# Differential attention's queries and keys turned by VectorE and DMA through DRAM, scores in rounded halves

## The chip, the cores and the metric

The kernel runs on one core of a Trainium2 chip. The metric is the device time of one execution in microseconds; smaller is better. Shown is the median of three executions.

## The reference

Two layers over 512 positions of width 1024, batch 1, all in float32. The second one (dilated windows and latent attention) isn't touched. The first is a retention branch and a differential attention branch behind one projection `w_in` of 1024 x 9216:

```python
h = rms_norm(x, norm_g);  z = h @ w_in            # q_d, k_d: 1024 columns each
qd = rms_norm(q_d.reshape(B, S, 8, 2, 64), diff_q_norm_g)   # 8 heads, two maps of 64
kd = rms_norm(k_d.reshape(B, S, 8, 2, 64), diff_k_norm_g)
# for each head, each block i of 128 queries, keys up to the block's end:
s = (qd * 64**-0.5) . kd - slope_h * dist;  s = -inf where key > query
p = softmax(s);  a = p[map 0] - lam * p[map 1];  o = a @ v_d
```

Then each head's output is normalised, gated, multiplied by `diff_w_o` and mixed with the retention branch.

## The kernel before

Positions are split in four tiles of 128 (`TT`). All projections are one stream on TensorE: 35 groups of up to eight slabs, a slab being 128 rows of a weight by 512 columns. A weight comes by DMA in chunks of two slabs (`chunk`, SyncE's queue, two buffers `raw`), ScalarE rounds it (`hi`, line 574, `w_hi`, float32r) and GpSimd takes the rest (`lo`, line 943, `w_lo`), each three slabs ahead, with four split slots. A product is then three rounded matmuls (`mm3`, lines 1708 to 1710): high by high, high by low, low by high. One slab is four of them, one for each tile: four slots. Every engine has a program of its own, written out in order, and they meet at semaphores.

The attention stage is the seven groups 13 to 19 (`in_diff`), 56 slabs or 224 slots v. Groups 10 and 11 before it project queries and keys of heads 0 to 3, groups 14 and 15 those of heads 4 to 7. Normalising: GpSimd squares, VectorE sums, takes the root and scales (`head_scale`, line 1239). Attention is written as generators, one per engine, over blocks n = 4h + i (head h, query block i). `diff_due(v)` says how many steps have been taken by slot v, and each slot calls `next` as often as that grows. A block's chain: TensorE's scores (`scores`, line 1808; per map j an fp32 matmul of 64 rows, 128(i+1) wide), VectorE adds bias and takes the maximum (line 1415, `s_max`), ScalarE takes exponentials (line 736, `s_exp`), VectorE the reciprocal (line 1406, `s_inv`), GpSimd scales map 1 (line 1030, `s_scaled`), VectorE combines (line 1438, `s_comb`), TensorE turns the probabilities (`turn_probs`, line 1833), VectorE copies them out (line 1424), TensorE makes the outputs (`outputs`, line 1820). `scores(n + 1)` are issued in iteration n, the turn of n in iteration n + 2. Both maps have one PSUM bank each.

Queries and keys come to their turned form on TensorE: `diff_turn` transposes four 128x128 tiles of `z_sb` into bank `A[2]` (line 1793), once for a head's queries and once for its keys, and ScalarE evicts them with gain and scale (`diff_queries`, `diff_keys`, lines 719 and 724). Each has a step of its own in iterations i = 1 and 2 of the head before:

```python
DIFF_FIRST, DIFF_SECOND, DIFF_THIRD, DIFF_LAST = 10, 116, 160, 208
```

so 86 steps, 36 of them up to slot 115, 22 in the next 44 slots and 28 in the last 48.

## Time and profile before

| | us |
|---|---|
| median of 3 executions (lowest, highest) | 908.52 (908.18, 908.61) |
| the profiled execution | 908.68 |
| its span, first to last instruction | 906.9 |
| TensorE busy in it | 896.1 |
| VectorE, ScalarE, GpSimd busy | 423.1, 397.3, 439.2 |
| DMA | 81.29 MB, 43564 packets |

What lies between the profiled execution's time and its span (1.8 us) is start and end around the program. Busy time of TensorE includes pipelining: a matmul's end is modelled, and starts are closer together than durations, so costs on TensorE are read from start to start. Engines other than TensorE may overlap it entirely. The granted clock is 1.00 throughout (2.4 GHz).

### The profile page before, as it was taken

Reading aid. Unit: us, or ns where it says so; the run is one execution under the profiler, and the core shown is the slowest. Engines: PE = TensorE matmul, PEld = TensorE weight load, DVE = VectorE, ACT = ScalarE, POOL = GpSimd, SP = SyncE. Lnnn points to the kernel's source line nnn. Section 1 sums busy time; section 2 is a strip of 40 time slices with the busy share of each in tenths; the row PEclk is TensorE's granted clock in tenths of the full one; section 3 lists DMA queues with packets and bytes.
Section 4 is the critical chain, followed back from the end, with each engine's and each line's share of the span. In section 5 each row is a group of like instructions: output and inputs, shape, how many; then the busy total and the mean of one; then the engine's idle time right before and its main releaser. Section 6 shows DMA issues by size and latency. Waiting matters only on the chain.

```text
span 906.9 us, 12615 instructions
## 1 busy us (share of the span) xinstructions
PE 896.1 (99%) x4648; PEld 712.7 (79%) x4648; DVE 423.1 (47%) x957; ACT 397.3 (44%) x872; POOL 439.2 (48%) x376
## 2 busy tenths in 40 slices
PE   9999999999999999999999999999999998999998
PEld 7878888888888877777777788889888765777776
DVE  3221251545114413467474455646648866543631
ACT  5533323333223344454554444244435774655531
POOL 4544436445446654646444444545458382234362
PEclk9999999999999999999999999999999999999999
DMA  8442222313333332122222233233433321011113
GB/s 317 152 104 77 65 70 79 108 59 105 96 104 100 97 90 73 48 72 70 69 55 63 70 116 139 93 108 96 120 101 105 94 87 53 25 47 47 47 47 116
DMA packets 43564, 81.29 MB, mean 90 GB/s; under 512 B 4416, under 2 KB 6208, under 8 KB 43504
## 3 DMA queue, kind: packets, MB, share of 16 engines
q1 hardware_dynamic: 42016, 79.95, 29.3%
q8 instruction: 37, 0.61, 0.3%
q10 hardware_dynamic: 1488, 0.55, 0.3%
q14 instruction: 23, 0.19, 0.1%
HBM read 78.36 MB, written 2.12 MB: 89 GB/s over the span
## 4 chain that ended last, share of the span: by engine, by line
PE 84%; DVE 8%; issue 3%; POOL 2%; DMA 2%; ACT 1%; SPq 0%; ACTq 0%; DVEq 0%; POOLq 0%
PE Z L1708 23%; PE Z L1710 22%; PE Z L1709 22%; PE A L1885 3%; PE A L1808 2%; PE A L1923 2%; PE A L1894 2%; PE A L1820 2%; DMA raw<-in_w_in 2%; DVE z_sb L1239 1%; PE A L1868 1%; POOL w_lo L943 1%; DVE rstd L1142 1%; PE A L1833 1%; PE A L1718 1%
## 5 line engine op out<-in xcount | busy, mean ns | idle before, releaser
L943 POOL TENSOR_TENSOR w_lo<-raw,w_hi 128x512 fp32r<-128x512 f32 (+1 forms) x262 | 345.3, 1325 | 443.9 <-ACT w_hi L574 442.6
L574 ACT CAST w_hi<-raw 128x512 fp32r<-128x512 f32 (+1 forms) x262 | 157.9, 614 | 293.7 <-PE Z L1710 259.7
L1708 PE MATMUL Z<-w_hi,hT_hi 128*128 128x512 f32 (+1 forms) x544 | 217.8, 400 | 0.1
L1710 PE MATMUL Z<-w_hi,hT_lo 128*128 128x512 f32 (+1 forms) x544 | 211.3, 388 | 0.0
L1709 PE MATMUL Z<-w_lo,hT_hi 128*128 128x512 f32 (+1 forms) x544 | 210.8, 388 | 0.0
L1708 PEld LDWEIGHTS Z<-w_hi,hT_hi 128*128 128x128 f32 x544 | 102.3, 188 | 27.8 <-issue 8.3
L1710 PEld LDWEIGHTS Z<-w_hi,hT_lo 128*128 128x128 f32 x544 | 102.1, 188 | 20.8
L1709 PEld LDWEIGHTS Z<-w_lo,hT_hi 128*128 128x128 f32 x544 | 102.4, 188 | 17.7
L1708 PE MATMUL Z<-hT_hi,w_hi 128*128 128x512 f32 x260 | 113.1, 435 | 0.3 <-DVE hT_lo L1174 0.3
L1710 PE MATMUL Z<-hT_hi,w_lo 128*128 128x512 f32 x260 | 102.1, 393 | 0.0
L1709 PE MATMUL Z<-hT_lo,w_hi 128*128 128x512 f32 x260 | 101.6, 391 | 0.0
L1708 PE MATMUL Z<-oT_hi,w_hi 128*128 128x512 f32 x160 | 63.0, 394 | 0.0
L1710 PE MATMUL Z<-oT_hi,w_lo 128*128 128x512 f32 x160 | 62.4, 390 | 0.0
L1709 PE MATMUL Z<-oT_lo,w_hi 128*128 128x512 f32 x160 | 62.3, 389 | 0.0
L1708 PEld LDWEIGHTS Z<-hT_hi,w_hi 128*128 128x128 f32 x260 | 49.3, 190 | 15.6 <-issue 7.7
L1710 PEld LDWEIGHTS Z<-hT_hi,w_lo 128*128 128x128 f32 x260 | 48.8, 188 | 10.8
L1709 PEld LDWEIGHTS Z<-hT_lo,w_hi 128*128 128x128 f32 x260 | 49.2, 189 | 7.5 <-issue 0.7
L736 ACT ACTIVATE x_sb<-x_sb,nmax 128x128 f32<-128x128 f32 (+3 forms) x64 | 35.4, 555 | 39.8 <-DVE nmax L1415 39.8
L1415 DVE CUSTOM_DVE_ANT_0 x_sb<-A,bias 128x128 f32<-128x128 f32 (+3 forms) x64 | 28.6, 483 | 49.8 <-PE A L1808 49.8
L785 ACT ACTIVATE sgd_sb<-sgd_sb,nmax 128x128 f32<-128x128 f32 (+3 forms) x64 | 35.7, 559 | 26.1 <-DVE nmax L1480 25.9
L1489 DVE COPY pT<-A 128x384 f32<-128x384 f32 (+2 forms) x40 | 22.3, 557 | 34.6 <-PE A L1894 34.4
L1221 DVE TENSOR_REDUCE stat<-bias 128x4 f32<-128x512 f32 (+1 forms) x16 | 11.0, 687 | 58.7 <-POOL bias L955 58.7
(239 smaller groups left out, 1298.7 us busy)
## 6 DMA issues: line engine op xcount, KB each, us to landing
raw<-in_w_in SPq DMA_DIRECT2D x91, 512.0 KB, 3.8
raw<-in_w_out SPq DMA_DIRECT2D x16, 512.0 KB, 3.6
raw<-in_ret_w_o SPq DMA_DIRECT2D x8, 512.0 KB, 3.2
raw<-in_diff_w_o SPq DMA_DIRECT2D x8, 512.0 KB, 3.3
x_sb<-in_x SPq DMA_DIRECT2D x4, 512.0 KB, 6.0
x_sb<-in_xT SPq DMA_DIRECT2D x4, 512.0 KB, 6.8
out<-x_sb SPq DMA_DIRECT2D x8, 256.0 KB, 2.9
raw<-in_w_in SPq DMA_DIRECT2D x4, 416.0 KB, 3.3
```

The costliest lines, as they stand in the source:

```text
L574: act.copy(w_hi[:, s % SPLIT_SLOTS, 0:width], raw[:, c % RAW_SLOTS, s - CHUNK_START[c], 0:width]).then_inc(hi_ready, 1)
L736: act.activation(p, p, ACT.Exp, bias=nmax[:, j, n:n + 1], scale=-1.0, accum_out=rsum[:, n, j:j + 1]).then_inc(s_exp, 1)
L785: act.activation(probs[:, n % 4, j, 0:w], probs[:, n % 4, j, 0:w], ACT.Exp, bias=nmax[:, j, n:n + 1], scale=-1.0, accum_out=rsum[:, n, j:j ...
L943: pool.tensor_tensor(w_lo[:, s % SPLIT_SLOTS, 0:width], raw[:, c % RAW_SLOTS, s - CHUNK_START[c], 0:width], w_hi[:, s % SPLIT_SLOTS, 0:wid ...
L1415: dve.tensor_tensor_reduce(diff_probs(j, n, w), A[j][:, score_columns(i, True)], bias[:, h % 2, S - w:S], -1.0, TOP, ALU.add, ALU.min, nma ...
L1489: dve.tensor_copy(turned_place(m, j), A[2][:, 0:P * (i + 1)].rearrange("p (b s) -> p b s", s=P)).then_inc(h_pt_out, 1)
L1708: pe.matmul(out, l_hi, r_hi, start=first, stop=False)
L1709: pe.matmul(out, l_hi, r_lo, start=False, stop=False)
L1710: return pe.matmul(out, l_lo, r_hi, start=False, stop=last)
L1808: pe.matmul(A[j][:, score_columns(i, True)], qT[rows, h % 2, P * i:P * (i + 1)], kT[rows, h % 2, 0:P * (i + 1)], start=True, stop=True).th ...
L1820: last = pe.matmul(A[3][:, DV * im:DV * (im + 1)], pT[:, 0, m % 2, kk], diff_values(hm)[:, kb, :], start=kb == 0, stop=kb == im)
L1885: pe.matmul(A[j][:, score_columns(i, shared)], qT[rows, slot, P * i:P * (i + 1)], kT[rows, slot, 0:P * (i + 1)], start=True, stop=True).th ...
```

## The change

The turn leaves TensorE. VectorE transposes each normalised 128x512 tile in squares of 32x32 (`turned_rows`, in between the scalings of `head_scale`) into `d_rows`, four tiles to a matrix of 512x512. SyncE writes that to DRAM (`rows_written`, in two parts, runs of 128 elements, which are 512 bytes), where it lies as rows of one feature; there are four such matrices (queries and keys, two halves). For each head SyncE reads queries and keys back (`queries_read`, `keys_read`), a map's 64 rows twice, into the upper and the lower 64 partitions. Within a row positions stand in an order that an access pattern mends (`in_order`, `by_squares`). VectorE multiplies the queries by both gains and the scale (`queries_gained`). ScalarE rounds queries and keys (`queries_high`, `keys_high`, two instructions each). In the lower 64 partitions of the queries VectorE puts what the rounding left (`queries_low`); GpSimd makes the low part of the keys (`keys_low`). A score is then two rounded matmuls of 128 rows: queries high and low stacked, by keys high, plus the same by keys low. All products of the halves are so summed.

The two steps per head for the turns fall away: 72 steps, 30 of them up to slot 139 and 42 in slots 140 to 207. Squares for the first half's matrices are made two to a slab in place of one; pieces of `head_scale` for the second half come one to a slot. SyncE does the writes and reads at fixed places of the queue of chunks, counted in slabs from the stage's start (`ROWS_OUT`, `QUERIES_IN`, `KEYS_IN`).

```diff
@@ -105,7 +105,8 @@
 XT_DMA = [0, 1, 2, 2, 3, 3, 4, 4]
 WARM = 4
-DIFF_FIRST, DIFF_SECOND, DIFF_THIRD, DIFF_LAST = 10, 116, 160, 208
+DIFF_FIRST, DIFF_SECOND, DIFF_LAST = 15, 140, 208
+DIFF_STEPS = 2 * (4 * H + 4)
 def diff_due(v):
@@ -113,10 +114,14 @@
     if v < DIFF_FIRST:
         return 0
     if v < DIFF_SECOND:
-        return 36 * (v - DIFF_FIRST + 1) // (DIFF_SECOND - DIFF_FIRST)
-    if v < DIFF_THIRD:
-        return 36 + 22 * (v - DIFF_SECOND + 1) // (DIFF_THIRD - DIFF_SECOND)
-    return min(86, 58 + 28 * (v - DIFF_THIRD + 1) // (DIFF_LAST - DIFF_THIRD))
+        return 30 * (v - DIFF_FIRST + 1) // (DIFF_SECOND - DIFF_FIRST)
+    return min(DIFF_STEPS, 30 + (DIFF_STEPS - 30) * (v - DIFF_SECOND + 1) // (DIFF_LAST - DIFF_SECOND))
+ROWS_OUT = ((-4, 0), (2, 4), (26, 28), (34, 36))
+QUERIES_IN = (0, 8, 14, 22, 30, 38, 42, 46)
+KEYS_IN = (6, 10, 16, 24, 36, 40, 44, 46)
...
+        qk_dram = nc.dram_tensor("qk_dram", [4, 512, S], F32)
         Z = [ctx.enter_context(nc.psum_tensor(f"Z{i}", [P, 512], F32)) for i in range(4)]
...
+        def diff_slot_of(h, j):
+            return 2 * (h % 2) + j
+        k_raw = pT[:, 1, :, :]
+        d_rows = sgd_sb[:, 0:4, :].rearrange("p w s -> p (w s)").rearrange("p (b t c) -> p b t c", t=TT, c=32)
+        def in_order(v):
+            return v.rearrange("p (a t c) -> p t a c", a=4, c=32)
+        def by_squares(v):
+            return v.rearrange("p (t a c) -> p t a c", a=4, c=32)
         def diff_probs(j, n, w):
...
@@ -488,6 +513,40 @@
             def x_turned(k, n):
                 src = a["xT"][P * k:P * (k + n), :].rearrange("(s p) c -> p s c", p=P)
                 sp.dma_start(xT[:, k:k + n, :], src).then_inc(xt_loaded[XT_DMA[k]], 16)
+            def rows_written(i, part):
+                v = qk_dram[:, :, :]
+                sp.wait_ge(rows_ready, TT * (i + 1))
+                b0, b1 = ((0, 4), (4, 16))[part]
+                for q in range(4):
+                    to = bass.AP(tensor=v.tensor, offset=(16 * i + b0) * 32 * S + P * q,
+                                 ap=[[S, 32], [32 * S, b1 - b0], [1, P]])
+                    rows = d_rows[32 * q:32 * (q + 1), b0:b1, :, :].rearrange("r b t c -> r b (t c)")
+                    sp.dma_start(to, rows).then_inc(rows_out[part], 16)
+            def read_twice(dst, i, w, landed):
+                v = qk_dram[:, :, :]
+                src = bass.AP(tensor=v.tensor, offset=(4 * i + w) * P * S, ap=[[S, DK], [DK * S, 2], [1, S]])
+                for lower in range(2):
+                    sp.dma_start(dst[DK * lower:DK * (lower + 1), :, :], src).then_inc(landed, 16)
+            def queries_read(h):
+                half, w = divmod(h, 4)
+                sp.wait_ge(rows_out[w > 0], 64 * (2 * half + 1))
+                if h:
+                    sp.wait_ge(q_lo, 2 * h)
+                read_twice(q_raw, 2 * half, w, q_in)
+            def keys_read(h):
+                half, w = divmod(h, 4)
+                sp.wait_ge(rows_out[w > 0], 64 * (2 * half + 2))
+                if h:
+                    sp.wait_ge(k_lo, 2 * h)
+                read_twice(k_raw, 2 * half + 1, w, k_in)
             def first_slab(k):
...
+                    for part in range(2):
+                        if SLAB0[g] + k - SLAB0[G_DIFF0] == ROWS_OUT[i][part]:
+                            rows_written(i, part)
+                for h in range(H):
+                    if SLAB0[g] + k - SLAB0[G_DIFF0] == QUERIES_IN[h]:
+                        queries_read(h)
+                    if SLAB0[g] + k - SLAB0[G_DIFF0] == KEYS_IN[h]:
+                        keys_read(h)
                 if g == G_DIFF_OUT + 1 and k == 0:
...
@@ -714,15 +782,22 @@
                                        A[2 + hh][:, :].rearrange("p (t e) -> p t e", t=TT), ACT.Copy,
                                        scale=qdec_c[:, h:h + 1]).then_inc(r_xe, 1)
-            def diff_queries(w):
-                act.wait_ge(qk_t, 2 * w + 1)
-                act.activation(qT[:, w % 2, :], diff_qk_bank(w, 0)[:, :], ACT.Copy,
-                               scale=cols[:, 35:36]).then_inc(qk_out, 1)
-            def diff_keys(w):
-                act.wait_ge(qk_t, 2 * w + 2)
-                act.activation(kT[:, w % 2, :], diff_qk_bank(w, 1)[:, :], ACT.Copy,
-                               scale=cols[:, 36:37]).then_inc(qk_out, 1)
+            def queries_high(h):
+                act.wait_ge(q_gained, h + 1)
+                if h >= 2:
+                    act.wait_ge(s_mm, 8 * (h - 1))
+                for j in range(2):
+                    act.activation(by_squares(q_both[:, diff_slot_of(h, j), :]), in_order(q_raw[:, j, :]), ACT.Copy,
+                                   scale=1.0).then_inc(q_hi, 1)
+            def keys_high(h):
+                act.wait_ge(k_in, 32 * (h + 1))
+                if h >= 2:
+                    act.wait_ge(s_mm, 8 * (h - 1))
+                for j in range(2):
+                    act.copy(by_squares(k_high[:, diff_slot_of(h, j), :]), in_order(k_raw[:, j, :])).then_inc(k_hi, 1)
             def diff():
...
                                            accum_out=rsum[:, n, j:j + 1]).then_inc(s_exp, 1)
-                    yield
-                    if i in (1, 2) and h + 1 < H:
-                        (diff_queries if i == 1 else diff_keys)(h + 1)
-                        yield
+                    if i == 1 and h + 1 < H:
+                        queries_high(h + 1)
+                    yield
+                    if i == 1 and h + 1 < H:
+                        keys_high(h + 1)
                     if i == 2 and n >= 6:
...
-                    diff_queries(0)
-                    diff_keys(0)
+                    queries_high(0)
+                if g == G_DIFF0 and k == 3:
+                    keys_high(0)
                 if g + 1 in TURNED and k >= 4:
                     turned(oT_hi[:, k - 4, :], turn_gain(g + 1, k - 4))
...
@@ -1010,6 +1086,14 @@
                 else:
                     last.then_inc(q_latent, 1)
+            def keys_low(h):
+                for j in range(2):
+                    pool.wait_ge(k_hi, 2 * h + j + 1)
+                    slot = diff_slot_of(h, j)
+                    pool.tensor_tensor(by_squares(k_low[:, slot, :]), in_order(k_raw[:, j, :]),
+                                       by_squares(k_high[:, slot, :]), ALU.subtract).then_inc(k_lo, 1)
             def diff_bias(h):
                 if h >= 2:
...
                     h, i = divmod(n, 4)
+                    if i == 2 and h + 1 < H:
+                        keys_low(h + 1)
                     if 1 <= n < N + 1:
                         m = n - 1
                         pool.wait_ge(s_inv, m + 1)
                         p1 = diff_probs(1, m, P * (m % 4 + 1))
                         pool.tensor_scalar(p1, p1, rinv[:, m, 1:2], lam[:, 0:1], ALU.mult, ALU.mult).then_inc(s_scaled, 1)
                     yield
-                    if i in (1, 2) and h + 1 < H:
-                        yield
                     if i == 2 and h + 1 < H:
                         diff_bias(h + 1)
...
+                    if g and g - 1 in HEAD_NORM and g >= G_LAYER2 and k < 7:
                         c0, t = HEAD_NORM[g - 1], k - 3
                         pool.wait_ge(z_by_act, act_evacs[g - 1] + t + 1)
-                        square(z_sb[:, t, c0:c0 + 512], 512, squares_2 if g >= G_LAYER2 else squares_1)
+                        square(z_sb[:, t, c0:c0 + 512], 512, squares_2)
+                    if g and g - 1 in HEAD_NORM and g < G_LAYER2 and k < 5:
+                        for t in (2 * k - 6, 2 * k - 5):
+                            c0 = HEAD_NORM[g - 1]
+                            pool.wait_ge(z_by_act, act_evacs[g - 1] + t + 1)
+                            square(z_sb[:, t, c0:c0 + 512], 512, squares_1)
...
@@ -1225,7 +1317,16 @@
                 buf = bufs[count["sq"] % len(bufs)]
                 sum_squares(stat[:, 8 * t:8 * t + 8], buf.rearrange("p (h e) -> p h e", h=8))
-            def head_scale(c0):
+            def turned_rows(c0, i, t):
+                dve.wait_ge(head_normed, TT * i + t + 1)
+                if i and t == 0:
+                    for part in range(2):
+                        dve.wait_ge(rows_out[part], 64 * i)
+                dve.transpose(d_rows[:, :, t, :], z_sb[:, t, c0:c0 + 512].rearrange("p (b c) -> p b c", c=32)
+                              ).then_inc(rows_ready, 1)
+            def head_scale(c0, rows=None):
                 dve.wait_ge(sq_used, count["sq"])
...
                                       ALU.mult).then_inc(head_normed, 1)
+                    if rows is not None and t:
+                        turned_rows(c0, rows, t - 1)
+                if rows is not None:
+                    yield
+                    turned_rows(c0, rows, TT - 1)
                 yield
...
@@ -1415,6 +1521,8 @@
                             dve.tensor_tensor_reduce(diff_probs(j, n, w), A[j][:, score_columns(i, True)],
                                                      bias[:, h % 2, S - w:S], -1.0, TOP, ALU.add, ALU.min,
                                                      nmax[:, j, n:n + 1]).then_inc(s_max, 1)
+                    if i == 2 and h + 1 < H:
+                        queries_low(h + 1)
                     if 0 <= n - LAG < N:
...
-                        yield
-                    yield
+                    if i == 0 and h + 1 < H:
+                        queries_gained(h + 1)
+                    yield
+            def queries_gained(h):
+                dve.wait_ge(q_in, 32 * (h + 1))
+                dve.tensor_scalar(q_raw[:, :, :], q_raw[:, :, :], cols[:, 35:36], None, ALU.mult).then_inc(q_gained, 1)
+            def queries_low(h):
+                low = slice(DK, P)
+                for j in range(2):
+                    dve.wait_ge(q_hi, 2 * h + j + 1)
+                    q = by_squares(q_both[low, diff_slot_of(h, j), :])
+                    dve.tensor_tensor(q, in_order(q_raw[low, j, :]), q, ALU.subtract).then_inc(q_lo, 1)
             def diff_slot(g, k, steps, norms):
                 v = TT * (KD * (g - G_DIFF0) + k)
+                if g == G_DIFF0 and k == 0:
+                    queries_gained(0)
+                if g == G_DIFF0 and k == 1:
+                    queries_low(0)
                 for t in range(TT):
                     if normed_in(g) and 2 <= TT * k + t <= 8 and t % 2 == 0:
                         head_sums(2 * k + t // 2 - 1, squares_d)
                     for _ in range(diff_due(v + t) - diff_due(v + t - 1)):
                         next(steps)
-                    if normed_in(g) and k in (3, 4):
+                    if normed_in(g) and 9 <= TT * k + t <= 17:
                         next(norms[g])
-                    if g == G_DIFF0 + 4 and k in (5, 6):
+                    if g == G_DIFF0 + 5 and k in (0, 1):
                         next(norms["first"])
                     if g == G_DIFF1 and k in (5, 6):
                         next(norms["second"])
...
+            link(dve.tensor_scalar(cols[:, 35:36], cols_in[:, 35:36], cols_in[:, 36:37], DK ** -0.5, ALU.mult, ALU.mult))
...
@@ -1782,31 +1910,22 @@
                                              start=True, stop=True)
                     last.then_inc(r_u, 1)
-            def diff_turn(w, i):
-                c0 = 1024 * i + P * w
-                if 4 * w - 4 + i > 0:
-                    pe.wait_ge(p_out, 4 * w - 4 + i)
-                if w == H // 2:
-                    pe.wait_ge(head_normed, 12 + 4 * i)
-                for t in range(TT):
-                    last = pe.transpose(diff_qk_bank(w, i)[:, P * t:P * (t + 1)], z_sb[:, t, c0:c0 + P], ident[:, :])
-                last.then_inc(qk_t, 1)
             def diff():
                 N = 4 * H
                 def scores(n):
                     h = n // 4
-                    pe.wait_ge(qk_out, 2 * h + 2)
+                    pe.wait_ge(q_lo, 2 * h + 2)
+                    pe.wait_ge(k_lo, 2 * h + 2)
                     if n:
                         pe.wait_ge(s_max, 2 * n)
                     for i in (0, 1) if n % 4 == 0 else (n % 4,):
                         for j in range(2):
-                            rows = slice(DK * j, DK * (j + 1))
-                            pe.matmul(A[j][:, score_columns(i, True)], qT[rows, h % 2, P * i:P * (i + 1)],
-                                      kT[rows, h % 2, 0:P * (i + 1)], start=True, stop=True).then_inc(s_mm, 1)
+                            slot, bank = diff_slot_of(h, j), A[j][:, score_columns(i, True)]
+                            q = q_both[:, slot, P * i:P * (i + 1)]
+                            pe.matmul(bank, q, k_high[:, slot, 0:P * (i + 1)], start=True, stop=False)
+                            pe.matmul(bank, q, k_low[:, slot, 0:P * (i + 1)], start=False, stop=True).then_inc(s_mm, 1)
                 def outputs(m):
```

## Rows read from the trace of the kernel before

**Rows 1.** The page's head: span, busy time, share, instructions of each engine.
```profile
span 906.9 us, 12615 instructions
PE 896.1 (99%) x4648; PEld 712.7 (79%) x4648; DVE 423.1 (47%) x957; ACT 397.3 (44%) x872; POOL 439.2 (48%) x376
```
**Rows 2.** Timeline of TensorE around a turn: start us, us, engine, line, operation.
```profile
329.77 0.39 PE L1708 MATMUL Z<-w_hi,hT_hi 128*128 128x512 f32 x1
...
332.94 0.39 PE L1710 MATMUL Z<-w_hi,hT_lo 128*128 128x512 f32 x1
333.18 0.60 PE L1793 MATMUL A<-ident,z_sb 128*128 128x128 f32 x4
333.53 0.48 PE L1708 MATMUL Z<-w_hi,hT_hi 128*128 128x512 f32 x1
333.84 0.40 PE L1709 MATMUL Z<-w_lo,hT_hi 128*128 128x512 f32 x1
```
**Rows 3.** Window 470 to 510: us, busy of PE, PEld, DVE, ACT, POOL; clock, DMA share, GB/s.
```profile
470.00:510.00 40.00, 39.91 (x211) 28.77 (x209) 22.05 (x72) 20.87 (x72) 17.30 (x20) 1.00 0.18 53
```
**Rows 4.** Waits of TensorE: engine line <- releaser, us in total, times, longest.
```profile
PE A L1793 <- DVE z_sb L1239: 0.9, 1, 0.9
PE A L1820 <- DVE o_sb L1431: 0.8, 1, 0.8
```
**Rows 5.** Timeline of TensorE around 384-wide scores.
```profile
462.80 0.40 PE L1710 MATMUL Z<-w_hi,hT_lo 128*128 128x512 f32 x1
463.13 0.92 PE L1808 MATMUL A<-kT,qT 64*128 64x384 f32 x4
...
464.31 0.40 PE L1709 MATMUL Z<-w_lo,hT_hi 128*128 128x512 f32 x1
```
**Rows 6.** Timeline of TensorE around 512-wide scores.
```profile
489.65 0.40 PE L1710 MATMUL Z<-hT_hi,w_lo 128*128 128x512 f32 x1
489.97 1.13 PE L1808 MATMUL A<-kT,qT 64*128 64x512 f32 x4
...
491.37 0.40 PE L1709 MATMUL Z<-hT_lo,w_hi 128*128 128x512 f32 x1
```
**Rows 7.** Timeline of TensorE: scores of blocks 0 and 1, then outputs.
```profile
493.54 0.93 PE L1808 MATMUL A<-kT,qT 64*128 64x128 f32 x8
494.39 0.49 PE L1820 MATMUL A<-z_sb,pT 128*128 128x128 f32 x2
```
**Rows 8.** Timeline of TensorE: 384-wide projections, nine starts apart.
```profile
688.98 0.33 PE L1708 MATMUL Z<-w_hi,cT_hi 128*128 128x384 f32 x1
...
690.57 0.33 PE L1708 MATMUL Z<-w_hi,cT_hi 128*128 128x384 f32 x1
```
**Rows 9.** Line L1239 (normalising): min/median/max ns, first and last start us.
```profile
L1239 DVE TENSOR_TENSOR z_sb<-z_sb,rstd x24: 677/684/1817, 289.3 to 709.7; 128x512 f32<-128x512 f32 x24
```
**Rows 10.** Timeline of VectorE: keys of the first half normalised.
```profile
311.74 3.62 DVE L1239 TENSOR_TENSOR z_sb<-z_sb,rstd 128x512 f32<-128x512 f32 x4
```
**Rows 11.** Timeline of TensorE: first projection matmul of the stage.
```profile
316.20 0.39 PE L1708 MATMUL Z<-w_hi,hT_hi 128*128 128x512 f32 x1
```
**Rows 12.** DMA issues of the page: count, KB each, median us to landing.
```profile
raw<-in_w_in SPq DMA_DIRECT2D x91, 512.0 KB, 3.8
```
**Rows 13.** Line L719 (evicting a turn): min/median/max ns.
```profile
L719 ACT ACTIVATE qT<-A,cols x8: 682/689/690, 319.7 to 482.7; 128x512 f32<-128x512 f32 x8
```
**Rows 14.** The page's groups: busy us, mean ns of one, idle before, releaser.
```profile
L943 POOL TENSOR_TENSOR w_lo<-raw,w_hi 128x512 fp32r<-128x512 f32 (+1 forms) x262 | 345.3, 1325 | 443.9 <-ACT w_hi L574 442.6
```
**Rows 15.** Groups of ScalarE, 470 to 510 us: the exponentials.
```profile
L736 ACT ACTIVATE x_sb<-x_sb,nmax 128x512 f32<-128x512 f32 (+3 forms) x18 | 10.3, 573 | 7.2 <-DVE nmax L1415 7.2
```
**Rows 16.** Same window, line L1708 alone: us, busy of PE and PEld (count).
```profile
470.00:510.00 40.00, 15.35 (x35) 6.61 (x35) 1.00 0.18 53
```
**Rows 17.** Timeline of VectorE: combining of a 384-wide block.
```profile
474.84 0.61 DVE L1438 SCALAR_TENSOR_TENSOR x_sb<-x_sb,rinv 128x384 f32<-128x384 f32 x1
```
**Rows 18.** Timeline of TensorE: that block's probabilities turned.
```profile
476.75 0.49 PE L1833 MATMUL A<-ident,x_sb 128*128 128x128 f32 x3
```

39 lines of the change are left out of this document (20 added, 19 removed).

## The prediction

> **What bounds the kernel now.** I read the page's head first: TensorE is busy for 896.1 us of a 906.9 us span, every other engine for less than half of it [rows 1]. A busy TensorE can still be waiting inside its pipeline, so next I looked at its timeline. Projection matmuls (128x512, three to one quarter of a slab) start one every 0.226 us: the first and the last row of the run in [rows 2] are 14 starts and 3.17 us apart. There is no gap in that stream, and in the windows of the attention stage TensorE is busy for 39.91 of 40 us at full clock [rows 3]. So inside the stage this change touches, the time is the sum of what TensorE issues, and work of the other four engines costs nothing until it makes TensorE wait. A piece of attention put between two projection matmuls costs: start of the second projection matmul after it, less start of the last one before it, less 2 x 0.226 us. I use that for every piece.
>
> The profiled execution took 908.68 us, 0.16 above the median of 908.52. I sum against 908.68 and take 0.16 off at the end.
>
> **What leaves TensorE: the turns.** `diff_turn` puts four transposes in, 16 times. In [rows 2] that is 333.84 - 332.94 - 0.45 = 0.45 us each, so 16 x 0.45 = 7.2 us. Nothing of it lay beside other TensorE work. One of them (at 425 us, head 4) also waited 0.9 us for VectorE's normalising [rows 4]. In the new order these keys are normalised over 9 slots that end at slab 28.3, and head 4's scores come near slab 35, so I count that wait as removed: 0.9 us.
>
> **What changes on TensorE: the scores.** Before, a head has three pieces of fp32 score matmuls. 384 wide: 464.31 - 462.80 - 0.45 = 1.06 us [rows 5]. 512 wide: 491.37 - 489.65 - 0.45 = 1.27 us [rows 6]. Blocks 0 and 1 together, followed directly by fp32 outputs: from 493.54 to 494.39 = 0.85 us [rows 7]. Sum 3.18 us. In the first two pieces about 0.2 us is entering and leaving (0.33 us from the last projection matmul where 0.226 is usual, and as much behind). After, each score is two rounded matmuls of the projection's own kind with 128 rows in place of 64: four each 128, 256, 384 and 512 wide. 512 wide is 0.226 us. 384 wide is (690.57 - 688.98) / 9 = 0.177 [rows 8]. The line through both gives 0.128 at 256 and 0.079 at 128; a 128-wide pass with a weight load of its own is seen in a turn: 333.53 - 333.18 = 0.35 us for four, 0.088 each [rows 2]. I take 0.088, since each new one loads weights too. A head is 4 x (0.088 + 0.128 + 0.177 + 0.226) = 2.48 us; entering and leaving fall away, because like follows like. Saved: 3.18 - 2.48 = 0.70 a head, 5.6 us for eight. Bounds: at 0.079 it is 5.9 us. From above, no rounded matmul narrower than 384 is in the trace: if both narrow widths cost what 512 does, 8 x (0.226 - 0.108) = 0.94 us a head more, 7.6 us in all; if 0.2 us twice a head stays at the edges, 3.2 us more. The term then lies between -5.2 and +5.9. The 128-wide row is nearest, hence 5.6.
>
> TensorE's sum: 7.2 + 0.9 + 5.6 = 13.7 us.
>
> **What is added elsewhere, and its cover.** VectorE: 16 transposes of 128x512; not in the trace. The nearest is the normalising of the same shape, 0.68 us in the median, up to 1.82 where something disturbs it [rows 9]. I take 0.68 and keep twice that as the upper bound: 11 to 22 us in all, four to a matrix, where VectorE has half of its time free.
>
> The start of the stage is the tight place. Today the normalising of the first half's keys starts at 311.74 [rows 10]; the squares now come two to a `w_lo`, two `w_lo` fewer in front, 2.6 us earlier. With four transposes between the scalings the rows are ready at 311.74 - 2.6 + 8 x 0.68 = 314.6. The stage's first projection matmul starts at 316.20 [rows 11], a slab is 12 x 0.226 = 2.7 us. SyncE waits for these rows at queue position 2, with the chunk of slabs 2 and 3 behind it. That chunk lands at 314.6 + 2 (the 256 KB written ahead, by estimate) + 3.8 (a 512 KB load, [rows 12]) = 320.4, and is split at 320.4 + 0.6 + 1.3 = 322.3; TensorE wants it at 316.2 + 5.4 = 321.6. Late by 0.7; with transposes at twice the price by 3.4. Then the keys of head 0: 2.5 MB stand in the queue up to their end (two chunks, 1 MB written, 512 KB read), at 512 KB in 3 to 4 us some 15 to 20 us from 314.6, less what overlaps; ScalarE copies (2 x 0.69, [rows 13]) and GpSimd subtracts (2 x 1.33, [rows 14]) at 330 to 334. Scores of head 0 come at slot 19, 316.2 + 20 x 0.68 = 329.8. I take 1.5 us of waiting for both together, between 0 and 5.
>
> The other three `rows_written` have cover: SyncE reaches position s when TensorE is near slab s - 7, and a chunk comes about 8 us before it would be missed; positions -4, 26 and 34 find their rows ready within 2 us. All writing and reading is 12 MB in 240 us, 50 GB/s beside the 53 of the windows' last column [rows 3].
>
> **The dense half.** Here the change moves work: blocks 15 to 35 now have the 68 slots from 140 to 208. Before, from 470 to 510 us, 9 blocks went by (18 exponentials, [rows 15]) with 35 slots [rows 16]: 4.44 us and 3.9 slots a block. 35 slots are 23.8 us, so attention pieces took 16.2 us, 1.8 a block. After: 1.8 - 0.22 (two turns in four blocks) - 0.18 (scores) = 1.4, and 3.24 slots x 0.68 = 2.2: 3.6 us a block. Load per block from [rows 3]: VectorE 22.05 / 9 = 2.45, ScalarE 2.32, GpSimd 1.92. Added per head on VectorE are `queries_gained` (128x1024, 0.7 to 1.4 us) and `queries_low` (2 x 0.68), some 0.6 a block, so 3.05 of 3.6 us. ScalarE makes four copies instead of two: +0.35, so 2.7. GpSimd: 2 x 1.33 / 4 = +0.66, less 0.2 for fewer `w_lo`, so 2.4. All fit, VectorE at 85%, but they are queues in order and wait for each other. The turn of a block's probabilities waits for VectorE's combining (`s_comb`), that for GpSimd's scaling (`s_scaled`), and in front of the scaling stands now `keys_low`, which waits for ScalarE's `keys_high`. Measured slack today in the tightest place: combining ends at 474.84 + 0.61 = 475.45 [rows 17], its turn starts at 476.75 [rows 18], 1.3 us. Following one head at 3.6 us a block, the slack of that turn comes out between -1 and +1 us once a head, and recovers in the next block. I take 0.4 us for each of five heads: 2 us. Bounds: 0; and, with GpSimd's 2 x 1.33 and one `w_lo` wholly in front, 4.0 - 1.3 = 2.7 us a head, 13.5 us.
>
> **Sum.** 908.68 - 13.7 + 1.5 + 2.0 = 898.5; less 0.16: 898.3 us.
>
> The Trainium skill speaks against the change (VectorE: DVE Perf Modes, "Rules for kernel authors"): a 128x128 turn belongs on TensorE where its result may land in PSUM, and VectorE turns only 32x32 blocks. By that rule the 7.2 us would be well spent: TensorE would save only the scores' 5.6 us and the time would be about 903. What the trace has of it, TensorE full and VectorE half idle, speaks the other way here; no row shows the VectorE turn itself.
>
> **The rivals.**
> *The dense half gives half of it back.* Stalls of 4 to 9 us where VectorE is at 85% and takes and head norms fall in between: 900.5 to 905.5, say 902.5. For it: one turn had only 1.3 us left at 4.4 us a block. Against: the loads fit with 15% over, and TensorE stalled 0.09 us in those 40. 0.17.
> *Narrow rounded matmuls cost like wide ones.* +7.6 us: 905.9. For it: none is shown. Against: time falls in proportion from 512 to 384. 0.06.
> *Slower: GpSimd's low halves of the keys hold every block of probabilities.* Place: `keys_low` ahead of the scaling, in seven heads. If the subtraction through a permuted pattern takes twice 1.33 us, the two are 5.3 us, with a `w_lo` 6.6, less 1.3 of slack 5.3 a head in the five dense ones and some 2 in others: 30 - 13.7, some 16 us slower at worst; 912 is half of the way. It decides from 3.9 us of delay a head. Against: GpSimd runs ahead of the scaling's need for most of a block. 0.08.
> *No gain: the queue of SyncE.* Slow transposes and writes in short runs hold the weights past their cover at each of four `rows_written`, by 3 us: 12 us in place of 1.5, 908.8. For it: the first half's keys are late by the sum above. Against: the other three are not. 0.05.
> Mine (894 to 900.5): 0.64.
>
> **How the numbers follow.** This kernel's measurement tells 0.2% (1.8 us) from no change. Faster: mine, the first two rivals and a part of the fourth, 0.88. Within 0.2%: 0.04. Slower: 0.08. Range: from all stalls at zero with the 0.079 price and the stage's second wait, 0.8 us [rows 4], gone (908.5 - 13.7 - 0.3 - 0.8 = 893.7, rounded down to 893.5) up to 905, which leaves out the narrow-matmul rival, the slower case, no gain and the top of the first.
>
> **What would show it.** No transposes of `z_sb` in fp32 from 319 to 488 us. A piece of scores 0.71 us at 384 and 0.90 at 512, and no 0.1 us edges round it. VectorE's transposes at 0.6 to 0.7 us. TensorE's waits in the stage (the waits view) sum to 2 to 5 us, named after `s_comb`'s writer or the low halves of keys. Span from the first projection of this stage to the last shorter by 10 us, and nothing changed before or behind. Wrong if: a 128-wide rounded matmul starts 0.2 us after the last; the waits for VectorE or GpSimd in the second half are above 8 us; or weights arrive late after `rows_written`.

## The result: 942.4 us, 3.7% slower

| | before, same chip | after |
|---|---|---|
| median of 4 (lowest, highest), us | 908.57 (908.18, 909.47) | 942.35 (936.63, 946.85) |
| profiled execution, its span, us | | 942.98, 940.8 |
| mean granted clock over the span | 1.000 | 0.984 |

The ratio is 1.0367, 95% interval 1.031 to 1.0424. I had forecast 898.3, faster. The page's head after, which answers to [rows 1]:

```profile
span 940.8 us, 12649 instructions
PE 899.9 (96%) x4584; PEld 726.9 (77%) x4584; DVE 467.0 (50%) x998; ACT 402.6 (43%) x887; POOL 467.7 (50%) x392
PEclk9999999999999989989998999999999999999999
```

The 64 transposes are gone (4648 to 4584 matmuls), yet TensorE is busy for longer, and its clock dips. The windows of the stage after (columns as in [rows 3]):

```profile
300.00:340.00 40.00, 33.99 (x142) 27.49 (x141) 16.84 (x29) 11.86 (x20) 22.40 (x18) 0.93 0.63 167
340.00:380.00 40.00, 39.42 (x180) 32.41 (x180) 17.69 (x46) 21.59 (x51) 21.44 (x20) 0.95 0.42 115
380.00:420.00 40.00, 32.92 (x150) 26.12 (x149) 24.46 (x56) 15.41 (x42) 23.86 (x21) 0.91 0.41 106
420.00:460.00 40.00, 33.50 (x158) 27.03 (x157) 27.58 (x63) 16.37 (x45) 22.69 (x21) 0.96 0.37 105
460.00:500.00 40.00, 33.08 (x175) 27.22 (x174) 27.71 (x68) 19.22 (x61) 20.80 (x21) 0.96 0.39 106
500.00:540.00 40.00, 34.76 (x177) 28.39 (x176) 29.14 (x77) 19.29 (x63) 21.76 (x21) 0.91 0.29 80
```

TensorE is idle for 5 to 7 of 40 us in five of six windows, and part of what it does issue runs at a lower clock. No other engine is full (VectorE 29 of 40 at most): they wait for each other. TensorE's timeline names the stalls (in brackets the idle time ahead of the row and what ended it). Of 16 such rows from 290 to 560 us, 31.8 us in all (1.7 before), the long ones:

```profile
324.45 0.79 PE L1836 MATMUL Z<-w_hi,hT_hi 128*128 128x512 f32 x1 [2.53 <-POOL w_lo L1019]
337.95 0.45 PE L1927 MATMUL A<-k_high,q_both 128*128 128x128 f32 x1 [3.48 <-POOL k_low L1094]
396.52 0.30 PE L1927 MATMUL A<-k_high,q_both 128*128 128x128 f32 x1 [2.58 <-DVE nmax L1521]
413.60 0.76 PE L1836 MATMUL Z<-w_hi,hT_hi 128*128 128x512 f32 x1 [3.77 <-ACT z_sb L660]
414.17 0.63 PE L1837 MATMUL Z<-w_lo,hT_hi 128*128 128x512 f32 x1
414.59 0.63 PE L1838 MATMUL Z<-w_hi,hT_lo 128*128 128x512 f32 x1
...
472.31 0.55 PE L1949 MATMUL A<-ident,x_sb 128*128 128x128 f32 x3 [2.86 <-DVE x_sb L1546]
492.42 0.47 PE L1836 MATMUL Z<-hT_hi,w_hi 128*128 128x512 f32 x1 [2.29 <-POOL w_lo L1019]
```

Behind the stall at 413.60 the projection matmuls start 0.42 us apart (414.17 to 414.59) where 0.226 is usual: half the clock, 1.2 in place of 2.4 GHz. Fine windows show its extent (same columns):

```profile
409.00:411.00 2.00, 0.83 (x5) 0.35 (x3) 0.76 (x3) 0.00 (x0) 0.56 (x1) 1.00 0.86 141
413.00:415.00 2.00, 1.40 (x3) 1.16 (x4) 0.32 (x1) 2.00 (x7) 1.65 (x2) 0.50 1.07 317
417.00:419.00 2.00, 2.00 (x6) 1.71 (x6) 0.00 (x0) 1.75 (x4) 1.21 (x1) 0.50 0.00 0
419.00:421.00 2.00, 2.00 (x9) 1.74 (x9) 0.69 (x1) 0.62 (x1) 2.00 (x3) 0.89 0.00 0
```

So the stall cost 3.8 us of idleness, and then nearly 6 us of work went at half the clock, some 3 us lost. Windows of 1 us over all the stalls show seven such stretches, behind those at 324, 338, 414, 435, 495, 508 and 527 us, 31 us together, so some 15 us lost. The account of the span, +33.9 us (940.8 - 906.9): turns -7.2; scores -4.2 (below); stalls +30.1; what is left, +15.2, is the clock's size (0.016 x 940.8 = 15.1).

**Two things that wait for the low halves.** One place after, in three views. VectorE makes head 2's low halves, and SyncE's read of head 3's queries has been waiting for them; the weights' chunk is queued behind that read:

```profile
384.97 2.72 DVE L1564 TENSOR_TENSOR q_both<-q_raw,q_both 64x512 fp32r<-64x512 f32 x2
```
```profile
387.76 1.24 SPq L533 DMA_DIRECT2D q_raw<-qk_dram  x2
389.04 0.59 SPq L511 DMA_DIRECT2D raw<-in_w_in  x1
```
```profile
395.80 0.62 ACT L642 CAST w_hi<-raw 128x512 fp32r<-128x512 f32 x1 [8.45 <-DMA raw<-in_w_in]
```

ScalarE, in its order, stands 8.45 us at the rounding of a slab that hasn't landed, and evictions and exponentials stand behind it. That is the first way. But TensorE's stall beside it, at 396.52 us, was ended by VectorE's maxima (`nmax`), and shows the second: behind the low halves and one copy VectorE stood 1.41 us until GpSimd had scaled, and then worked without a gap, the pieces of a head norm among it, until the maxima were done.

```profile
389.42 1.25 DVE L1546 SCALAR_TENSOR_TENSOR x_sb<-x_sb,rinv 128x256 f32<-128x256 f32 x1 [1.41 <-POOL x_sb L1116]
```

In e1, below, where the reads of heads 1 to 7 are left out, the stall at this place is 3.65 us long:

```profile
393.25 0.44 PE L1927 MATMUL A<-k_high,q_both 128*128 128x128 f32 x1 [3.65 <-DVE nmax L1521]
```

SyncE's own waits add up over the execution to:

```profile
SPq L540 <- DVE q_both L1564: 91.0, 7, 19.6
SPq L526 <- DVE sgd_sb L1326: 45.6, 4, 13.8
SPq L548 <- POOL k_low L1094: 2.9, 1, 2.9
```

Seven reads of queries wait 91 us for the low halves, four writes 45.6 us for the squares. These are waits of SyncE and not yet losses: with the reads left out (e1) it waits longer for a buffer of weights to come free, 742.5 us instead of 640.5. The prices on VectorE and GpSimd:

```profile
L1564 DVE TENSOR_TENSOR q_both<-q_raw,q_both 64x512 fp32r<-64x512 f32 x16 | 20.4, 1313 | 13.8 <-ACT q_both L791 13.5
L1326 DVE STREAM_TRANSPOSE sgd_sb<-z_sb 128x512 f32<-128x512 f32 x16 | 10.7, 689 | 0.0
L1556 DVE TENSOR_SCALAR q_raw<-q_raw,cols 128x1024 f32<-128x1024 f32 x8 | 7.0, 870 | 0.0
```
```profile
L1094 POOL TENSOR_TENSOR k_low<-pT,k_high 128x512 fp32r<-128x512 f32 x16 | 24.8, 1574 | 0.8 <-ACT k_high L800 0.8
```

### The profile page after: what moved, and what is told of

It is laid out like the page before. It is cut to its first block, busy times and chain, and to the rows that moved or that the text cites. A ratio compares the mean times of both kernels' runs of the same rounds, so it can differ in the third digit from the quotient of the medians.

```text
span 940.8 us, 12649 instructions
## 1 busy us (share of the span) xinstructions
PE 899.9 (96%) x4584; PEld 726.9 (77%) x4584; DVE 467.0 (50%) x998; ACT 402.6 (43%) x887; POOL 467.7 (50%) x392
## 4 chain that ended last, share of the span: by engine, by line
PE 67%; DVE 10%; POOL 7%; DMA 6%; issue 4%; ACT 4%; SPq 1%; ACTq 0%; DVEq 0%; POOLq 0%
PE Z L1836 18%; PE Z L1838 18%; PE Z L1837 18%; DMA raw<-in_w_in 6%; POOL w_lo L1019 3%; PE A L1998 3%; PE A L2007 2%; PE A L2036 2%; DVE z_sb L1340 2%; POOL k_low L1094 2%; PE A L1981 1%; ACT w_hi L642 1%; DVE q_both L1564 1%; SPq L526 1%; POOL x_sb L1116 1%
## 5 line engine op out<-in xcount | busy, mean ns | idle before, releaser
L1836 PE MATMUL Z<-w_hi,hT_hi 128*128 128x512 f32 (+1 forms) x544 | 218.9, 402 | 10.6 <-ACT z_sb L660 8.1
L1837 PE MATMUL Z<-w_lo,hT_hi 128*128 128x512 f32 (+1 forms) x544 | 213.5, 392 | 0.0
L1546 DVE SCALAR_TENSOR_TENSOR x_sb<-x_sb,rinv 128x128 f32<-128x128 f32 (+3 forms) x32 | 27.9, 873 | 39.4 <-POOL x_sb L1116 39.1
```

Of the source, the lines that this page charges most:

```text
L1546: dve.scalar_tensor_tensor(p0, p0, rinv[:, m, 0:1], diff_probs(1, m, wm), ALU.mult, ALU.add).then_inc(s_comb, 1)
L1836: pe.matmul(out, l_hi, r_hi, start=first, stop=False)
L1837: pe.matmul(out, l_hi, r_lo, start=False, stop=False)
```

## The experiments

"Stalls" is TensorE's idle time from 290 to 560 us in pieces of 0.25 us or more, added up in the timeline, each stall once; before has 1.7, after 31.8. Ratios are to the kernel before on the same chip (908.28 to 909.82).

| run | us | ratio (95%) | stalls | clock |
|---|---|---|---|---|
| e1 reads out | 932.15 | 1.0240 (1.0216, 1.0263) | 19.9 | .987 |
| e2 reads late | 942.74 | 1.0360 (1.0342, 1.0378) | 32.5 | .985 |
| e3 before, new pace | 911.38 | 1.0021 (1.0012, 1.0031) | 2.8 | 1.000 |
| e4 reads on ScalarE's queue | 936.31 | 1.0301 (1.0284, 1.0318) | 26.9 | .987 |
| e5 low halves out | 926.57 | 1.0201 (1.0174, 1.0228) | 23.4 | .987 |
| e6 both out | 917.01 | 1.0096 (1.0079, 1.0113) | 18.4 | .996 |
| e7 start later | 937.87 | 1.0327 (1.0293, 1.0360) | 30.0 | .980 |
| e8 heads 0 to 3 only | 915.23 | 1.0079 (1.0064, 1.0094) | 10.5 | .996 |
| e9 low halves behind | 958.87 | 1.0539 (1.0523, 1.0556) | 42.5 | .975 |
| e10 the same, reads out | 929.99 | 1.0223 (1.0208, 1.0238) | 23.0 | .987 |
| e11 heads 1 to 3 only | 914.66 | 1.0054 (1.0039, 1.0069) | 8.0 | .994 |
| e12 turn alone | 916.58 | 1.0076 (1.0059, 1.0093) | 8.9 | .994 |
| e13 turn alone, writes later | 910.39 | 1.0003 (0.9993, 1.0014) | 6.4 | .996 |
| e14 turn alone, 3 writes out | 902.37 | 0.9926 (0.9911, 0.9941) | 1.6 | .998 |
| e15 the change, writes later | 938.84 | 1.0328 (1.0303, 1.0354) | 28.7 | .983 |
| e16 as e13, first slot 18 | 906.80 | 0.9974 (0.9963, 0.9985) | 4.5 | 1.000 |
| e17 as e13, first slot 21 | 904.28 | 0.9946 (0.9933, 0.9960) | 3.0 | 1.000 |
| e18 as e13, first slot 15 | 902.97 | 0.9933 (0.9921, 0.9946) | 2.5 | 1.000 |

The same stalls by what ended them, in us. "Weights" is `w_lo` or an eviction of ScalarE that stood behind a late rounding; "attention" is VectorE's maxima and combining.

| run | weights | first head's keys | attention | other |
|---|---|---|---|---|
| after | 12.7 | 3.5 | 14.1 | 1.5 |
| e1 reads out | 3.5 | 1.3 | 15.1 | 0 |
| e2 reads late | 10.0 | 3.2 | 19.2 | 0 |
| e5 low halves out | 11.9 | 3.4 | 7.3 | 0.8 |
| e10 low halves behind, reads out | 4.4 | 2.9 | 15.8 | 0 |
| e12 turn alone | 7.0 | 0 | 1.9 | 0 |
| e18 turn alone, writes later | 0 | 1.0 | 1.6 | 0 |

### The queue, the pace

**e1.** Reads of heads 1 to 7 left out; all heads work on head 0's.

```diff
-                for h in range(H):
+                for h in range(1):
                     if SLAB0[g] + k - SLAB0[G_DIFF0] == QUERIES_IN[h]:
```

> Leaves out: queries and keys are read back for head 0 only; heads 1 to 7 work on what lies in the buffers, so the output is not the reference's, and all other instructions stay. Theory Q (the reads wait in SyncE's queue for VectorE's and GpSimd's low halves, 91 us of waiting, and hold the weights behind them): without them the weights come in time and the time falls to 903 to 915, with only the first 8 us of stalls at the stage's start left. Theory D (VectorE and GpSimd are too full in the dense half, whoever reads): the reads cost no engine anything, so it stays above 930.

932.15: 10 of the 34 us go, 19.9 us of stalls stay although SyncE no longer waits for a read. The reads are a part of the cause, not the whole: without them the stalls for weights fall from 12.7 to 3.5 us, and those for VectorE stay (14.1 and 15.1). Undisturbed score pieces can be read here:

```profile
514.36 0.22 PE L1927 MATMUL A<-k_high,q_both 128*128 128x128 f32 x1
514.42 0.28 PE L1928 MATMUL A<-k_low,q_both 128*128 128x128 f32 x1
...
515.16 0.28 PE L1928 MATMUL A<-k_low,q_both 128*128 128x256 f32 x1
515.28 0.39 PE L1939 MATMUL A<-z_sb,pT 128*128 128x128 f32 x2
```

Eight narrow rounded matmuls take 515.28 - 514.36 = 0.92 us, 0.06 to 0.17 each. So the rival of dear narrow matmuls falls, from this run's trace.

**e2.** Reads later: queries at 0, 8, 16, 26, 34, 42, 46, 50, keys at 6, 10, 18, 26, 36, 42, 46, 50.

```diff
-QUERIES_IN = (0, 8, 14, 22, 30, 38, 42, 46)
+QUERIES_IN = (0, 8, 16, 26, 34, 42, 46, 50)
```

> Same work; queue positions of the reads moved back so that SyncE reaches them when TensorE is about at the slab in which the low half of the head before is due: queries at 0, 8, 16, 26, 34, 42, 46, 50, keys at 6, 10, 18, 26, 36, 42, 46, 50. Theory Q: the waits for the low halves of queries fall from 91 to under 25 us and the time to 912 to 925; in the dense half a read then comes too late for its head now and again. Theory D: nothing changes by more than 5 us, above 937.

942.74, with 32.5 us of stalls: no gain, and yet SyncE's waits for the low halves fell from 91.0 to 8.5 us. Theory Q had that right and the time wrong. VectorE now waits for queries that come late instead (14.4 us), and the stalls for maxima and combining grow by 5 us:

```profile
SPq L540 <- DVE q_both L1564: 8.5, 2, 6.6
```
```profile
DVE q_raw L1556 <- DMA q_raw<-qk_dram: 14.4, 3, 4.9
```

**e3.** The kernel before, with the pace and norm slots of the change alone.

```diff
-DIFF_FIRST, DIFF_SECOND, DIFF_THIRD, DIFF_LAST = 10, 116, 160, 208
+DIFF_FIRST, DIFF_SECOND, DIFF_LAST = 15, 140, 208
```

> The kernel before with the new pace alone: 36 of its 86 steps up to slot 139 and 50 in the 68 slots after, first norms of heads one group later, no other part of the change. Theory D: 915 to 925, the dense half stalls by itself. Theory Q: 907 to 911, the pace alone costs at most 2 us.

911.38, +1.9 us. The new pace by itself costs hardly anything with the old work. What the added work costs at that pace this run doesn't show.

**e4.** Reads of heads 2 to 7 issued on ScalarE's DMA queue, behind its own copies.

```diff
+                    if i == 3 and h + 2 < H:
+                        queries_on(act, h + 2)
```

> Same work; reads of heads 2 to 7 are issued by ScalarE on its own DMA queue, after the exponentials of the last block of a head, where the low halves are already made; SyncE's queue holds only weights and rows written, and the reads of heads 0 and 1. Theory Q: 905 to 918; ScalarE pays about 0.6 us an issue, four a head, and the reads come 1 block before they are needed, some 2 us of waiting a head in the dense half. Theory D: above 930.

936.31, 6 us better, though the two ratios' intervals touch (1.0284 to 1.0318 against 1.031 to 1.0424), and far above the 905 to 918 of theory Q. Taken out of the weights' queue, the reads seem to cost less, but most of the loss stays.

### The low halves

**e5.** The low halves of heads 2 to 7 cover 32 of 512 columns only; the rest of the correction is left out. **e6** is e5 and e1 together.

```diff
+                    if h >= 2:
+                        q, src = q[:, 0:1, 0, :], src[:, 0:1, 0, :]
                     dve.tensor_tensor(q, src, q, ALU.subtract).then_inc(q_lo, 1)
```

> Leaves out: the low halves of queries (VectorE) and keys (GpSimd) of heads 2 to 7 are made for 32 of 512 columns only, so those heads' scores are not the reference's; reads, copies, matmuls and waits all stay. Theory L (the two subtractions of the low halves run side by side, 2.9 us on VectorE and 3.4 us on GpSimd in the run without reads, in front of the scaling and the combining, and TensorE waits for these): most of the second half's stalls go, and SyncE's reads are released a little sooner; 918 to 928 of the 942. Theory Q (SyncE's queue): the reads stay where they are, 935 or more.

> Leaves out both: reads of heads 1 to 7, and the low halves of heads 2 to 7 but for 32 columns. Theory L with Q: what is left is the start of the stage and the norms, 905 to 914. If neither holds the time (theory P: the pace and VectorE's other work), above 922.

926.57 and 917.01. Low halves alone -16, reads alone -10, both -25: the two causes nearly add up, and 8.7 us over the kernel before on that chip remain that belong to neither. In e5 SyncE still waits 83.2 us for `q_lo` and the stalls for weights stay (11.9); those for maxima and combining halve, 14.1 to 7.3. So the low halves cost mainly by their own time on VectorE and GpSimd, not by what they hold in the queue.

**e9.** Low halves put behind the scaling (GpSimd) and the combining (VectorE) in their step. **e10** is e9 with the reads of heads 1 to 7 left out.

```diff
-                    if i == 2 and h + 1 < H:
-                        queries_low(h + 1)
                     if 0 <= n - LAG < N:
...
                                                  ALU.add).then_inc(s_comb, 1)
+                    if i == 2 and h + 1 < H:
+                        queries_low(h + 1)
```

> Same work, other order: in iteration i = 2 GpSimd scales the probabilities first and makes the low half of the keys then, and VectorE makes the low half of the queries after the combining instead of before the copy. Theory L (the low halves stand in front of the scaling and the combining): TensorE's waits for the combining in the second half go, 925 to 935 against 942. Against it: the low halves take the same time wherever they stand and delay the next step as much, 939 or more.

> The order of e9 on the kernel of e1 (reads of heads 1 to 7 left out, output not the reference's). Against e1's 932: theory L 918 to 926; the other, 930 or more.

958.87, 17 us slower than the change; without reads 929.99, about e1's 932.15. So without reads it hardly matters whether low halves hold the probabilities or follow them: in e10 no stall is left at the combining (4.9 us in e1), but those at the maxima are 15.8 us instead of 10.3. With reads the order matters, for the low halves now let the next read, and the weights behind it, go later: e9 less e10 is 29 us, and in e9 SyncE's waits for them grow:

```profile
SPq L540 <- DVE q_both L1564: 110.7, 7, 22.2
```

### Which heads, which place

**e7.** Second write, first two reads of keys and first step later.

```diff
-ROWS_OUT = ((-4, 0), (2, 4), (26, 28), (34, 36))
+ROWS_OUT = ((-4, 0), (4, 6), (26, 28), (34, 36))
-KEYS_IN = (6, 10, 16, 24, 36, 40, 44, 46)
+KEYS_IN = (8, 12, 16, 24, 36, 40, 44, 46)
-DIFF_FIRST, DIFF_SECOND, DIFF_LAST = 15, 140, 208
+DIFF_FIRST, DIFF_SECOND, DIFF_LAST = 24, 140, 208
```

> Same work; keys of the first half are written at queue positions 4 and 6 instead of 2 and 4, read at 8, rounded at slab 5, and the first scores come at about slot 28 instead of 19. The waits at 324 us (2.5) and 338 us (3.5) go and with them the clock's fall in 300 to 340 us: 5 to 9 us less than 942 if the steps that then come closer together up to slot 139 cost nothing; same as 942 if the loss only moves.

937.87: the stall at 324 us is gone, the one for the first keys has grown from 3.5 us at 338 to 4.8 at 340, and the intervals of the two ratios overlap. **e8** turns heads 0 to 3 the new way, with e7's start, and 4 to 7 on TensorE with the old scores and nearly the old pace; **e11** turns heads 1 to 3 only the new way.

```diff
-                for h in range(H):
+                for h in range(4):
                     if SLAB0[g] + k - SLAB0[G_DIFF0] == QUERIES_IN[h]:
```

> A kernel with the whole computation: heads 0 to 3 by VectorE, DRAM and rounded halves with the later start of e7, reads where their buffers are free; heads 4 to 7 by TensorE's turns and fp32 scores as in the kernel before, its pace in the second half. TensorE saves 8 turns (3.6 us) and four heads of scores (2.8 us). Theory L: four blocks' time is about twice as long here, so the low halves are hidden: 903 to 907 against 909 before. If the losses do not come from the dense half, it is slower than before, 912 or more.

> The whole computation. The new way for heads 1 to 3 alone, low halves behind as in e9; head 0 and heads 4 to 7 turned on TensorE as before; only the blocks of heads 1 to 3 are written out (rows at queue positions 0 and 8), so that neither the stage's start nor its dense half depends on the road through DRAM. TensorE saves 6 turns (2.7 us) and three heads of scores (2.1 us). If the losses lie only at the start and in the dense half: 903 to 906 against 909. If VectorE's transposes, the copies and GpSimd's halves cost even with room around them: 908 or more.

915.23 and 914.66. The new way in the loose half alone costs 7 and 5 us over the kernel before on the same chip, instead of 34, and still isn't a gain.

### The turn alone

**e12.** The turn by squares and DMA stays; scores are the old ones (64 rows, fp32), with no low halves, gain or second copy, and one read for each map pair into two buffers. The computation is whole.

```diff
-                    sp.wait_ge(q_lo, 2 * h)
-                read_twice(q_raw, 2 * half, w, q_in)
+                    sp.wait_ge(q_hi, h - 1)
+                read_once(q_raw[:, h % 2, :], 2 * half, w, q_in[h % 2])
```

> The whole computation; the turn's part of the change without the scores' part: VectorE's transposes, the writes, one read of 128 rows per head into one of two buffers, one ScalarE copy each for queries and keys that puts positions in order, and scores as fp32 matmuls of 64 rows as before; pace and queue positions of the change. No gain multiplication, no low halves, no second copies. TensorE saves the turns alone, 7.2 us. Theory L: 905 to 912, the start's stalls of about 8 us with clock being what is left. Theory P (the pace and the queue are the loss, not the halves): 918 or more.

916.58, in between: the turn alone loses 7 us. (e6's 917.0 is another sum, with the rounded scores in it.) No read waits, but four writes do:

```profile
SPq L526 <- DVE sgd_sb L1319: 43.7, 4, 13.4
```
```profile
395.60 1.94 SPq L526 DMA_DIRECT2D qk_dram<-sgd_sb  x4
397.58 0.44 SPq L511 DMA_DIRECT2D raw<-in_w_in  x1
```
```profile
401.82 0.62 ACT L641 CAST w_hi<-raw 128x512 fp32r<-128x512 f32 x1 [4.58 <-DMA raw<-in_w_in]
```

The chunk goes out behind the wait and four issues of 0.48 us each, and ScalarE stands 4.6 us; TensorE's stall at 403.17 us (2.49) ends with the eviction behind that rounding.

**e14.** Three of the four writes left out; all heads read the first matrix.

```diff
             def rows_written(i, part):
+                if i:
+                    return
```

> This is the run with the turn alone (VectorE squares, DMA, fp32 scores), with the writes of three of the four matrices left out: all heads read both queries and keys out of the first matrix, so what is computed is not the reference's; SyncE waits for the squares of the first matrix alone. Theory W (SyncE's waits for the squares of the other three and the time to issue their twelve short-run DMAs are what the turn alone lost): the stalls at 325, 403 and 437 us go, TensorE's waits in the stage fall from 8.9 us to under 3, the clock is 1.00 and the time comes to 901 to 905 (908.5 less 7.2 for the turns, plus 1.9 for the pace). Rival S (the loss is the spread of the reads, copies and squares over the other engines): 912 or more.

902.37: theory W holds. All that the turn alone loses comes with the three writes, their waits and issues together.

**e13.** The writes one chunk later in the queue, nothing left out.

```diff
-ROWS_OUT = ((-4, 0), (2, 4), (26, 28), (34, 36))
+ROWS_OUT = ((-4, 0), (4, 6), (28, 30), (36, 38))
-KEYS_IN = (6, 10, 16, 24, 36, 40, 44, 46)
+KEYS_IN = (6, 10, 16, 24, 38, 40, 44, 46)
-DIFF_FIRST, DIFF_SECOND, DIFF_LAST = 15, 140, 208
+DIFF_FIRST, DIFF_SECOND, DIFF_LAST = 24, 140, 208
```

> The turn alone, whole computation, with SyncE's writes two slabs (one chunk of weights) later in its queue for the second and both second-half matrices, and the first head's keys and first step eight to nine slots later. Theory W: the weights are no longer late where the writes stand, the stalls at 325, 403 and 437 us shrink to under 1 us each, and the time comes to 902 to 907, below the kernel before. Rival S: 913 to 918, as with the writes where they were. In between: a wait of SyncE for rows is only moved, one stall goes and another appears (as when the start of the whole change was moved later).

910.39, level with before. The three stalls behind writes are gone, but for 0.4 us; one is new:

```profile
390.70 1.65 PE L1911 MATMUL A<-kT,qT 64*128 64x128 f32 x8 [4.09 <-DVE nmax L1514]
```

**e15.** The whole change with e13's positions.

> The whole change with the same later positions of its writes (the start as in the run with the later start, plus both second-half matrices two slabs later). If the writes' waits are a separate part of the loss: 942 less 6 to 12, 930 to 936. If the reads' waits for the low halves take up whatever is gained in SyncE's queue: 936 to 942.

938.84. What was worth 6 us in the turn alone is worth 3 or 4 here, and that is not clear of noise (1.0303 to 1.0354 against 1.031 to 1.0424). The stalls for weights halve (6.5 us), those for maxima and combining grow to 16.4.

**e16, e17, e18.** e13 with the first step from slot 18, 21 or 15 (the first keys copied at slab 4, 5, 4).

```diff
-DIFF_FIRST, DIFF_SECOND, DIFF_LAST = 24, 140, 208
+DIFF_FIRST, DIFF_SECOND, DIFF_LAST = 15, 140, 208
```

> The turn alone with the later writes of its queue positions, whole computation; attention's first step from slot 18 in place of 24 and the first head's keys copied at slab 4 in place of 5. With the later writes one stall of 4.1 us stood at 390 us, where VectorE does the nine pieces of a head norm with its four transposes in one go (382 to 389 us) between two of its attention steps; in the run with the writes left out, first step at slot 15, there was none. If that stall comes from how the norm's slots 9 to 17 fall between the steps, another first slot moves it off: waits of TensorE in the stage under 4 us, 904 to 907, below the kernel before by 0.3% or more. If it belongs to VectorE's work itself: 908 to 911, no change from before.

> As the run with the first step from slot 18, but from slot 21 and the keys at slab 5. Same two outcomes: 904 to 907 if the position of the steps makes the stall, 908 to 911 if VectorE's work itself does.

> As the run with the first step from slot 18, but from slot 15, where the run with the writes left out had no stall at 390 us. If the first head's keys, which come after a part of the writes at position 4, are not late for slot 19: 904 to 907. If they are (at most 3 us and the clock behind it): 908 to 912, with the stall near 330 us.

906.80, 904.28, 902.97: how the norm's pieces fall between the steps, not the amount of VectorE's work, made the stall at 390. e18 beats both kernels, by 0.67% (0.54 to 0.79%) the one before, as fast as e14 where most of the writes are missing. Since e18 does all the writes, neither their issue nor their data costs anything there; their place in the queue did. SyncE still waits 24.4 us at them, a little over half of e12's, and its fullest window of VectorE leaves TensorE busy:

```profile
SPq L526 <- DVE sgd_sb L1319: 24.4, 4, 8.7
```
```profile
380.00:420.00 40.00, 39.41 (x199) 30.47 (x198) 31.97 (x74) 16.76 (x45) 22.95 (x21) 1.00 0.37 107
```

## Why the prediction was wrong

**Turns, -7.2.** Right: e14 and e18 stand 7.2 and 6.4 us under the kernel before on their chips. With e3's 1.9 for the pace it would have been 5.3; that price doesn't show here.

**Scores, -5.6.** The right way, a quarter too much. A 512-wide piece costs 357.68 - 356.32 - 0.45 = 0.91 us (0.90 forecast), from these rows after:

```profile
356.32 0.39 PE L1838 MATMUL Z<-w_hi,hT_lo 128*128 128x512 f32 x1
356.54 0.39 PE L1927 MATMUL A<-k_high,q_both 128*128 128x512 f32 x1
...
357.68 0.39 PE L1837 MATMUL Z<-w_lo,hT_hi 128*128 128x512 f32 x1
```

384 wide is 499.93 - 498.65 - 0.45 = 0.83 (0.71), blocks 0 and 1 0.92 (0.86, read in e1): 2.66 a head for 3.18, so 4.2 us in all. The edges that were to fall away are still there at 384.

```profile
498.65 0.40 PE L1838 MATMUL Z<-hT_hi,w_lo 128*128 128x512 f32 x1
...
499.93 0.40 PE L1837 MATMUL Z<-hT_lo,w_hi 128*128 128x512 f32 x1
```

**VectorE's squares, 0.68.** Right: 0.689. The Trainium skill's rule against them (VectorE: DVE Perf Modes, "Rules for kernel authors") would have left the turn where it was; e18 shows that the turn on VectorE pays here once its writes stand in the right place, so the trace's argument held against the rule in that version, but not in the change as a whole.

**"A chunk comes about 8 us before it would be missed; positions -4, 26 and 34 find their rows ready within 2 us."** This is the first step that failed. SyncE stood 45.6 us at four writes, up to 13.8. At the start, where I took 1.5 us (0 to 5), TensorE stalled 2.53 us for weights and 3.48 us for the first keys. I took the slab that TensorE would be at for SyncE's time, but not that SyncE waits at the write from the moment the chunk before has gone. In the turn alone this is worth 14 us: 916.6 (e12) less 902.4 (e14), against 1.5 forecast. The rival "no gain: the queue of SyncE", 0.05 at 908.8, had the mechanism and 12 of these us.

**The reads in SyncE's queue.** Not priced at all. `queries_read` waits for `q_lo` of the head before, in front of the weights. I named what queues behind ScalarE, VectorE and GpSimd, and gave SyncE's queue the writes only. Without the reads 10 us go (e1), and e9 less e10 is 29 us when the low halves come later. It is not the waiting time that counts: e2 took 82 of the 91 us of waits away and gained nothing, while the stalls for maxima and combining grew by 5 us.

**"The dense half", 2.0 us.** The second step that failed, and the largest error: the low halves are worth 16 us (e5). I had the kind of wait right, probabilities and maxima that come late because VectorE and GpSimd are queues in order, but took 0.4 us for each of five heads. TensorE stalled 14.1 us for maxima and combining, 10.6 of them from 430 us on, where more than 8 was to be a sign of being wrong, with single stalls of up to 2.86 us. The pace is not it (1.9 us, e3, with the old work). One mis-sized part is `queries_low`, taken at 2 x 0.68 a head: it measured 1.31 each on average (0.68 to 1.79), on half of the partitions, and `keys_low` 1.57 where I took 1.33. After, seven heads' pairs on VectorE ran beside work of GpSimd and took 2.37 to 3.11 us; the one that ran while GpSimd was idle (3.58 us, up to 522.10) took 1.29:

```profile
520.65 1.29 DVE L1564 TENSOR_TENSOR q_both<-q_raw,q_both 64x512 fp32r<-64x512 f32 x2
```

So working side by side goes with the higher price in all eight heads; no run moved the one away from the other on purpose.

My slower rival had the sign and the engines, but not its conditions: it wanted 5.3 us for the pair of `keys_low`, which took 3.1, and put the harm in its place ahead of the scaling. With the low halves behind the scaling and the reads out (e10) the stalls at the combining are gone and the time is the same, for the maxima wait instead. That speaks against the place, not against the time that low halves take.

**The clock.** No term: some 15 of the 34 us. Before, with 1.7 us of stalls, it stood at 1.00 and no row warned of it.

What stays open: how the 16 us of the low halves divide between VectorE's and GpSimd's, which no run left out one at a time; how much of the reads' 10 us is their wait, their issue or their late landing; what the 8.7 us are made of that e6 leaves, beside the writes; and whether stacked scores on e18's positions with the reads off SyncE's queue would gain their 4.2 us, which was not tried.
